# A decoder block with 32 experts on one core: TensorE's program written out for all runs of the experts

## What is computed

```python
def expert_block(args):
    xb, e = args
    u = xb @ w_up[e] + b_up[e]                       # 1024 -> 2048
    glu = jnp.minimum(u[:, :D_FF], SWIGLU_LIMIT)
    lin = jnp.clip(u[:, D_FF:], -SWIGLU_LIMIT, SWIGLU_LIMIT)
    act = glu * jax.nn.sigmoid(SWIGLU_ALPHA * glu) * (lin + 1.0)
    return act @ w_down[e] + b_down[e]               # 1024 -> 1024
```

## Time and profile before

| | |
|---|---|
| median of 3 runs | 1632.55 us (1628.65 to 1633.89) |
| the profiled execution | 1628.29 us, of which 1626.4 us are the span from the first to the last instruction |
| mean granted clock of TensorE | 0.977 of full speed |
| PE busy | 1525.5 us (94% of the span) |
| DVE, ACT, POOL busy | 32%, 15%, 11% |
| DMA over the span | 468.69 MB, mean 288 GB/s |
| the experts' part | from about 544 us to 1602 us |

### The profile page before, as it was taken

The page is one execution under the profiler, slowest core; times in us unless marked ns, Lnnn a source line. Parts: engine busy times, 40 slices in busy tenths (PEclk is TensorE's granted clock), DMA queues, the critical chain, the costliest instruction groups (busy, mean ns, idle before and its releaser), DMA issues.

```text
span 1626.4 us, 28870 instructions
## 1 busy us (share of the span) xinstructions
PE 1525.5 (94%) x11139; PEld 649.6 (40%) x11139; DVE 524.9 (32%) x1368; ACT 248.7 (15%) x558; POOL 182.7 (11%) x186
## 2 busy tenths in 40 slices
PE   7999899999999889999899999999999899998993
PEld 3444466545545433433333333333333333333331
DVE  3224345331114553323322242233222422242232
ACT  3013333312111011101010011001100111011012
POOL 1000000070010001120111101111021110201101
PEclk9999999999999899999999999999999999999997
DMA  6211031052102788999999999999999999999996
GB/s 236 103 52 52 1 136 72 1 164 89 52 26 104 297 323 334 385 396 411 382 409 409 399 415 372 410 402 411 415 383 408 388 415 401 399 417 393 413 409 241
DMA packets 87790, 468.69 MB, mean 288 GB/s; under 512 B 12690, under 2 KB 12742, under 8 KB 38416
## 3 DMA queue, kind: packets, MB, share of 16 engines
q1 hardware_dynamic: 75960, 443.68, 67.5%
q0 software_dynamic: 11632, 23.08, 5.5%
q10 hardware_dynamic: 72, 0.02, 0.0%
HBM read 454.81 MB, written 17.56 MB: 290 GB/s over the span
## 4 chain that ended last, share of the span: by engine, by line
PE 80%; DMA 11%; DVE 4%; issue 3%; ACT 1%; ACTq 0%; POOL 0%; DVEq 0%; POOLq 0%; SPq 0%
PE bank L819 29%; PE bank L760 24%; PE bank L853 11%; DMA ring<-in_w_down 7%; PE bank L863 4%; DMA arena<-h_rows,arena 3%; PE bank L803 1%; PE bank L791 1%; PE bank L1016 1%; PE bank L999 1%; PE bank L779 1%; PE bank L1042 1%; PE bank L887 1%; PE bank L943 1%; PE bank L795 1%
## 5 line engine op out<-in xcount | busy, mean ns | idle before, releaser
L819 PE MATMUL bank<-ring,arena 128*32 128x512 f32 x5504 | 618.4, 603 | 1.3 <-DMA ring<-in_w_up 1.1
L819 PEld LDWEIGHTS bank<-ring,arena 128*32 128x32 f32 x5504 | 186.9, 111 | 385.7 <-issue 351.0
L853 PE MATMUL bank<-ring,arena 128*32 128x512 f32 x2048 | 254.6, 593 | 5.6 <-DMA ring<-in_w_down 5.5
L760 PE MATMUL bank<-ring,actT 128*128 128x512 f32 x448 | 198.6, 599 | 0.1
L1713 DVE TENSOR_SCALAR tokA<-bank 64x512 f32<-64x512 f32 x64 | 43.7, 683 | 384.2 <-PE bank L819 383.2
L853 PEld LDWEIGHTS bank<-ring,arena 128*32 128x32 f32 x2048 | 91.5, 110 | 123.8 <-issue 39.7
L656 POOL DMA_INDIRECT arena<-h_rows,arena x31 | 33.3, 1075 | 865.5 <-DVE arena L1684 840.1
L760 PEld LDWEIGHTS bank<-ring,actT 128*128 128x128 f32 x448 | 84.4, 193 | 98.7 <-issue 98.0
L863 PE MATMUL bank<-ring,arena 128*32 128x512 f32 x704 | 106.5, 592 | 0.0
L1298 ACT ACTIVATE tokA<-tokA 128x512 f32<-128x512 f32 x32 | 20.2, 630 | 459.1 <-DVE tokA L1713 459.1
L760 PE MATMUL bank<-actT,ring 128*128 128x512 f32 x192 | 83.5, 593 | 0.0
(11 more groups left out here) (330 smaller groups left out, 1273.4 us busy)
## 6 DMA issues: line engine op xcount, KB each, us to landing
ring<-in_w_up SPq DMA_DIRECT2D x256, 1024.0 KB, 10.9
ring<-in_w_down SPq DMA_DIRECT2D x128, 1024.0 KB, 10.9
ring<-in_w_in SPq DMA_DIRECT2D x12, 1024.0 KB, 12.2
ring<-in_w_ck SPq DMA_DIRECT2D x4, 1024.0 KB
ring<-in_w_out SPq DMA_DIRECT2D x4, 1024.0 KB, 7.5
ring<-in_w_cv SPq DMA_DIRECT2D x4, 1024.0 KB
ring<-in_w_cq SPq DMA_DIRECT2D x4, 1024.0 KB, 7.3
ring<-in_w_co SPq DMA_DIRECT2D x4, 1024.0 KB, 7.5
```

The source lines that it names most:

```text
L760: mm = pe.matmul(o, lhsT, rhs, start=(k == 0), stop=(k == KT - 1))
L819: mm = pe.matmul(bank[g][32 * t:32 * t + 32, :], lhsT, w[:, 512 * t:512 * t + 512], start=False, stop=(k == KT - 1))
L853: mm = pe.matmul(bank[3][rr:rr + 32, :], hTA[:, k % 4, g, k // 4, :], w[:, 512 * t:512 * t + 512], start=False, stop=(k == KT - 1))
```

## The change

On TensorE alone, the loop of nine turns is replaced by the same 27 iterations written out by Python; run numbers and all semaphore counts in them become constants. The matmuls, their order and their waits are the same. DVE, ACT, POOL and SP are untouched and keep their loops.

```diff
--- before.py
+++ after.py
@@ -1089,11 +1089,8 @@
                     rows_T(r + 2)
                 down(r, r, 2 * UP_CHUNKS)
 
-            for n in range(LOOP_FROM):
+            for n in range(LAST - 1):
                 iteration(Run(n))
-            with pe.Fori(0, LOOP_TURNS) as turn:
-                for u in range(3):
-                    iteration(Run(LOOP_FROM + u, turn))
             iteration(Run(LAST - 1), more=False)
             hidden_T(Run(LAST))
             down(Run(LAST), Run(LAST), UP_CHUNKS)
```

## The result

The written-out kernel takes 1621.05 us in the median of four runs (1620.8 to 1624.92), against 1632.76 us for the kernel before (four runs, 1628.65 to 1633.89): a ratio of 0.9938, with a 95% interval of 0.9916 to 0.9961. That is faster by 11.7 us. The forecast was 1622.0 us. The profiled execution took 1621.0 us with a span of 1619.2 us, 7.2 us less span than before; the forecast for it had been 1617.8 and 1615.9 us, so this single execution fell 3.2 us short of it.

What follows compares the result with a forecast made beforehand. The prediction took the DMA weight stream as the bound, with PE having slack. Idle bytes 9.3 us plus remainder 1.2 us, other terms 0, gave 10.5 us: 1632.55 - 10.5 = 1622.0 us, range 1609 to 1631 us.

Steps and rivals of the forecast that it cites:

- The bound: In the nine turns DMA's weight stream bounds, about 96.8 us in turn 4; PE itself needs 92.4 us.
- The idle bytes, 9.3 us: Behind PE's back edges the ring fills and queues run dry; 3.89 MB lost at 0.420 MB/us, 9.3 us to regain.
- the remainder, 1.2 us: Queue restart and gather bursts behind the five slow edges, a quarter of a microsecond each, 1.2 us to regain.
- the slack of 4.4 us: PE's spare time per turn against DMA, in which a back edge of 3.6 us mostly fits.
- The second way to the number: Check by turn length, the slower of PE and DMA: 2 x 2.4 + 3 x 1.4 = 9.0 us lost at slow-clock edges.
- Instruction loading, 0: PE's loop body is already reloaded each turn, so writing it out changes between 0 and minus one microsecond; taken as 0.
- From the profile to the median: Profiled execution forecast at 1617.8 us; the median's 4.26 us distance above it kept, giving 1622.0 us.
- The marks: Trace signs foretold: no line 803 issue waits, clock 1.00, DMA share 1.01 or more, chunk waits about 34 us.
- the wait for gathered rows stays: PE's wait for gathered rows, 4.4 us in eight pieces, was to remain unchanged inside PE's spare time.
- (a): Rival: PE was the bound, all 39.4 us come back, 1593 us; halfway form 1610 us; chance beyond forecast 0.12.
- (b): Rival: nothing comes back, the memory-bound weight stream idles elsewhere; gain 0 to 4.9 us, 1630 us, chance 0.18.
- (c): Rival: PE's straight code can't be loaded fast enough through full DMA engines; slower, 1651 us, chance 0.06.

Runs made afterwards that it cites:

- 1: Written-out code with PE stopped artificially where the eight back edges had been: five register loads each, 1628.09 us, ratio 0.9992; two loads each, 1619.1 us, 0.9944.
- 5: Half of each expert chunk's weight bytes left unloaded, in the kernel before (1586.42 us) and in the written-out kernel (1570.36 us).
- 6: Written-out code without column tiles 2 and 3 of w_up's matmuls in chunks 0 to 6, all DMAs kept: 1616.44 us, ratio 0.9912.
- 2: Kernel before with PE's loop kept and its back edge hinted: 1612.79 us, ratio 0.9902; run again 1612.69 us, beside 1620.29 us for the written-out code.
- 3: Kernel before with a hinted PE loop of nine iterations in the body and three turns: 1621.8 us, ratio 0.9944.

## Why the prediction was right, step by step

*The bound.* Right, and shown from both sides: adding a little to PE's time leaves the whole as it is (the short stops in 1), taking bytes away shortens the turns to PE's own need (5). That need is 91.7 us, against my 92.4 us. Leaving matmuls out (6) was to show it too, and does not.

*The idle bytes, 9.3 us, and the remainder, 1.2 us.* Right in kind and size: the artificial stops, 28.3 us in place of 29.1 us and with six slow stretches in place of five, put 9.0 us back (1), and the short stops, inside the slack of 4.4 us, nothing. The 9.0 us hold both terms; no run parts them. It was right to price a stop by what the stream loses behind it and not by its length: 29.1 + 10.3 us of PE's time were worth a quarter of that. Two readings behind the 9.3 us were weaker than they looked. The second way to the number took 96.3 us for DMA, for which no row is given; with the 96.8 us of turn 4 it gives 2 x 1.9 + 3 x 0.9 = 6.5 us. And the lost bytes do not lie behind slow edges alone: the edge at 1374.1 us had the full clock, and the stream ran at 362 GB/s behind it.

```profile
1374.10:1384.10 10.00, 10.00 (x103) 3.59 (x107) 1.40 (x9) 0.60 (x1) 2.05 (x2) 1.00 0.98 362
```

*Instruction loading, 0.* Here the reasoning was incomplete. I saw that the loop reloads its body, and priced only what the written-out code might add. Queue 8 fell from 107 to 91 packets; at the 0.14 us that 2 and 3 give for each, these 16 would be worth 2.2 us, which is an estimate. The direct comparison is the run with the long stops against the kernel before: 91 and 107 packets with nearly equal stops, 1.2 us apart, and its interval (0.9979 to 1.0004) holds no difference. So the term may be nothing or a few microseconds. The far larger part, the 56 packets that stay in the written-out code, did not occur to me.

*From the profile to the median.* In the profiled executions the gain was 7.3 us, in the medians 11.7 us, and on a later chip 1630.44 - 1620.29 = 10.2 us in the medians. The forecast of 10.5 us lies among them, but that it came within 1 us of the median of the after kernel is in part luck: the kernel before had a profiled execution 4.5 us below its median, and I carried this distance over to the kernel after, whose profiled one lies on its median. The loop's runs scatter more, and those with a higher mean clock tend to be shorter: on one later chip 1625.6 us at 0.981 and 1634.6 us at 0.974. But the order is loose (1628.5 us at 0.973 on that chip, 1629.3 us at 0.981 on another). That the number of edges with a low clock makes this scatter is likely and not shown: only one execution of the kernel before has a trace.

*The marks.* Issue waits ahead of line 803 gone, clock at 1.00, and 35.5 us of waits for weights against 34 us foretold: as written. The turns of 94.8 to 98.9 us go slightly beyond the 95 to 98 foretold. A DMA share of 1.01 or more in every 10 us from 790 us on did not come: to 1580 us eight of 79 such stretches lie below it, the lowest at 0.97.

```profile
1070.00:1080.00 10.00, 10.00 (x104) 4.99 (x100) 3.53 (x18) 1.97 (x3) 0.00 (x0) 1.00 0.97 373
```

Wrong was that the wait for gathered rows stays: it fell from 4.4 to 0.8 us. PE now waits for chunks of w_up ahead of it, and the rows are probably there by then.

*The rivals.* (a) PE as the bound is refuted by 5, by the short stops of 1 and by the time itself, 1621 us and not 1593 us. (b) no gain: refuted by the interval. (c) straight code that can't be loaded in time: one issue wait of 0.6 us in the whole stretch. But (c) pointed at the right thing from the wrong side. The loading doesn't hold PE up; PE's longer waits for weights in 2 say that it holds the weights up.

## What to carry to other kernels

Ask of each stall what the engine that is really full does meanwhile: stops well inside the slack of the engine that makes them were free here, and longer ones cost what the bound stream lost. Ahead of writing a loop out, try to keep its body in instruction memory and hint its edge: here that took the stall away and the loading as well, while the written-out code was 7.6 us slower with 56 packets more on DMA engines that the weights want. Ahead of leaving work out to test a bound, see in the trace that the engine's time really falls: half of the column tiles took as long as all of them. And set the profiled execution beside the other runs before a difference of two profiles is read: here it was 7.3 us where the medians gave 10.2 and 11.7 us.

## What the runs showed of the hardware

- At a back edge of PE whose code is loaded again, PE stood still for 3.6 us on average with the DMA engines full (share 1.0), for 1.75 us (0.9 to 2.8) with a share of 0.7, and under the hint for nothing that the waits show.
- With the hint a body of about 880 matmuls and as many weight loads stays in PE's instruction memory: 35 packets in place of 107 over the whole kernel. Without the hint the same body was loaded again in each turn. Why the unhinted loop throws away what would fit was not tried.
- With 56 instruction packets of 16 KB more in a saturated stream the kernel took 7.6 us longer, 0.14 us each. The same bytes in packets of half a KB on another queue cost 1.3 us for 60 times 16 KB, 0.02 us each, which is not told apart from nothing.
- Matmuls with 32 columns of weights stand side by side in the array: 16 of them, two column tiles of four, took 3.60 us where 32 took 3.61 to 3.81 us.
- Behind a stop of 3.3 to 3.8 us the granted clock fell to its lower level, 1.2 GHz, behind five of eight edges and six of the eight artificial stops, with means of 0.70 to 0.86 over the next 10 us; behind the eight stops of 1.6 us the next 10 us were all at 1.00, though it fell once later in a turn (a mean of 0.98 from 1364 to 1462 us).
